# Feed-forward products of a hybrid trunk step by seven block products instead of eight: all of layer 4, the last chunk of layers 1 to 3

## Chip, cores and metric
One NeuronCore of one Trainium2 chip. The metric is the device time of one execution in microseconds (us), the median of several runs. An engine is named PE (TensorE, the matrix unit), ACT (ScalarE), DVE (VectorE), POOL (GpSimd) or SP (SyncE, which here only issues loads).

## What is computed
640 tokens (512 of a sample, 128 of a prompt) of width 1024 pass through four layers. Each has a mixer (short convolution, pooling, attention, short convolution) and a feed-forward part, both behind a norm with a modulation (shift, scale, gate) that comes from a conditioning vector. The part that the change touches:

```python
def swiglu(h, w_in, w_out):
    g, u = jnp.split(h @ w_in, 2, axis=-1)
    return (jax.nn.silu(g) * u) @ w_out
...
hp = modulate(rms_norm(xp, norm2_w[i]), mod_p[3], mod_p[4])
xp = xp + mod_p[5] * swiglu(hp, ffn_in_w[i], ffn_out_w[i])
```

`w_in` is 1024 x 5632, so there are 22 tiles of 128 gate columns and 22 of up columns: 22 pairs a layer.

## The kernel before
**Layout.** Features lie on the 128 partitions, tokens along the free axis; `h` has 8 rows of 640 tokens and two extra columns, the product of which with the weights gives the bias (642 = 320 + 322 columns). Every fp32 operand is kept as a sum of two fp32r parts, hi and lo, and a product is three passes: hi·hi, hi·lo, lo·hi (`products`, L464 and L465).

**Units and quads.** A unit is one 128-column tile of weights over 8 rows of h: 8 rows x 3 passes x 2 halves of the tokens = 48 matmuls into two PSUM banks. Its weights arrive by SP's queue in one of four raw buffers (512 KB), ACT copies them to hi (`split_hi`, L872), DVE subtracts to get lo (`split_lo`, L1236), into one of two slots. Four units make a quad. In `step(q, j)` ACT and DVE make the unit two ahead once unit j is done, since it reuses that unit's slot. Even units of a feed-forward quad are gates, odd ones are ups: `scaled_out` (L1312) multiplies a result by the inverse rms, `gate` takes silu on ACT, `times` (L1323) multiplies the two, and `g_hi_of` (L884) and `g_lo_of` (L1250) split the result for the second product.

**Chunks.** The 22 pairs go in chunks of 8, 8 and 6 pairs. Behind each chunk come two output quads (`out_quad`, 8 units), in which DVE adds gate times product to the residual x (L1360, three pieces). PE may start the unit after the next only when DVE has emptied its banks (`freed[slot]`).

**Modulation.** The next layer's modulation is computed on DVE beside the feed-forward part of layers 1 to 3: dot products of 128 x 1024 tiles (`ada_sum`, L1264), in triples of three tiles with two vectors each. POOL loads the tiles, each one once DVE has used up the tile before in its buffer (`load_ada`). In an output quad of those layers each step of DVE carries three sums (`ada_twice`, triples=2). That is POOL's only work in the kernel before, apart from a few memsets at its start.

**Order.** Each engine runs its own written-out list and is in order: a wait at the head of the list holds all behind it. In the quad before a feed-forward part (`out_quad` with squares, layer 4: after the convolution) each step also squares the row (L940), adds it to the sum of squares (L1408) and folds the norm's gain into a row of h: `fold_hi` on ACT (L927), `fold_lo` on DVE (L1389). The rms itself is taken by `rms_of` (L944) and `inverse_rms` (L1420).

Layers are counted 1 to 4 in the text and 0 to 3 in the code.

## Time and profile before
| | us |
|---|---|
| median of 3 runs (2665.64 to 2666.2) | 2665.91 |
| the profiled execution | 2665.85 |
| its span, first to last instruction | 2664.2 |
| PE busy in the span | 2651.6 (100%) |
| DVE busy | 1718.7 (65%) |
| ACT busy | 862.8 (32%) |
| POOL busy | 94.0 (4%) |

The profiled execution takes 1.65 us more than its span, and lies 0.06 us under the median. Busy time of PE merges matmuls that overlap: the duration of one (some 310 ns) is its way through the array, and the distance from one start to the next is what a matmul costs. On DVE and ACT too an instruction's duration ends somewhat after the next one can start.

### The profile page before, as it was taken

The numbers are of one execution on the slowest core, as the hardware profiler recorded it, in microseconds if no ns is written. First come the engines' busy times: TensorE is split into PE (matmuls) and PEld (weight loads), VectorE is DVE, ScalarE is ACT, GpSimd is POOL, SyncE is SP. The second block draws the span as 40 slices with busy tenths as digits, with TensorE's granted clock in tenths as the row PEclk, the third lists the DMA queues.
The fourth block names the chain that finished last, engine by engine and source line by source line (L and its number), as shares of the span: only waits on it lengthen the run. The fifth ranks groups of instructions, "written<-read, shape, count | busy, mean of one in ns | idle before, by whom it ended". The sixth has DMA issues, their size and how long they took to land.

```text
span 2664.2 us, 45828 instructions
## 1 busy us (share of the span) xinstructions
PE 2651.6 (100%) x17638; PEld 2581.8 (97%) x17638; DVE 1718.7 (65%) x2908; ACT 862.8 (32%) x1185; POOL 94.0 (4%) x185
## 2 busy tenths in 40 slices
PE   9999999999999999999999999999999999999998
PEld 5999999999999999999968999999999999999998
DVE  5898778686587777746675778676465554334345
ACT  4223332322342122125665431322332233233122
POOL 0000001000000000000000001000000000000000
PEclk9999999999999999999999999999999999999999
DMA  8443345344223444422002235443122212222212
GB/s 308 142 146 138 127 140 174 124 162 132 77 85 129 161 144 134 142 67 86 33 13 88 96 133 174 132 144 119 64 87 71 79 64 79 79 71 71 79 65 70
DMA packets 85604, 294.95 MB, mean 111 GB/s; under 512 B 10112, under 2 KB 13312, under 8 KB 85248
## 3 DMA queue, kind: packets, MB, share of 16 engines
q1 hardware_dynamic: 60016, 200.74, 22.5%
q0 software_dynamic: 25488, 92.81, 10.4%
q8 instruction: 70, 1.15, 0.2%
q14 instruction: 30, 0.25, 0.0%
HBM read 290.63 MB, written 2.88 MB: 110 GB/s over the span
## 4 chain that ended last, share of the span: by engine, by line
PE 96%; DVE 2%; ACT 1%; DMA 1%; issue 0%; DVEq 0%; ACTq 0%; SPq 0%
PE ps L464 45%; PE ps L465 45%; PE ps_x L678 1%; PE ps L654 1%; PE ps L810 1%; PE ps_sum L665 1%; DMA mix<-in_ada_head 1%; DVE w_lo L1236 1%; PE ps L761 0%; ACT w_hi L872 0%; PE ps L535 0%; PE ps_sum L640 0%; DVE g_lo L1250 0%; ACT g_hi L884 0%; DVE tmp L1312 0%
## 5 line engine op out<-in xcount | busy, mean ns | idle before, releaser
L1236 DVE TENSOR_TENSOR w_lo<-raw,w_hi 128x1024 fp32r<-128x1024 f32 (+2 forms) x359 | 429.1, 1195 | 634.0 <-ACT w_hi L872 632.0
L872 ACT ACTIVATE w_hi<-raw 128x1024 fp32r<-128x1024 f32 (+2 forms) x359 | 371.9, 1036 | 973.2 <-PE ps L465 967.1
L464 PE MATMUL ps<-h_hi,w_hi 128*128 128x320 f32 x1888 | 590.2, 313 | 0.7 <-DVE h_lo L1396 0.7
L465 PE MATMUL ps<-h_lo,w_hi 128*128 128x322 f32 x1888 | 586.5, 311 | 0.0
L464 PE MATMUL ps<-h_hi,w_lo 128*128 128x320 f32 x1888 | 586.3, 311 | 0.0
L465 PE MATMUL ps<-h_hi,w_lo 128*128 128x322 f32 x1888 | 585.8, 310 | 0.0
L465 PE MATMUL ps<-h_hi,w_hi 128*128 128x322 f32 x1888 | 584.6, 310 | 0.0
L464 PE MATMUL ps<-h_lo,w_hi 128*128 128x320 f32 x1888 | 583.9, 309 | 0.0
L1264 DVE CUSTOM_DVE_ANT_0 ps_x<-ada_w,cond 128x1024 f32<-128x1024 f32 x354 | 435.9, 1231 | 28.5 <-DVE tmp L1312 13.2
L465 PEld LDWEIGHTS ps<-h_hi,w_hi 128*128 128x128 f32 x1888 | 359.0, 190 | 0.6
L465 PEld LDWEIGHTS ps<-h_hi,w_lo 128*128 128x128 f32 x1888 | 358.2, 190 | 0.0
L464 PEld LDWEIGHTS ps<-h_hi,w_hi 128*128 128x128 f32 x1888 | 354.7, 188 | 1.5 <-DVE h_lo L1396 0.8
L465 PEld LDWEIGHTS ps<-h_lo,w_hi 128*128 128x128 f32 x1888 | 355.9, 189 | 0.0
L464 PEld LDWEIGHTS ps<-h_hi,w_lo 128*128 128x128 f32 x1888 | 355.0, 188 | 0.0
L464 PEld LDWEIGHTS ps<-h_lo,w_hi 128*128 128x128 f32 x1888 | 353.9, 187 | 0.0
L464 PE MATMUL ps<-g_hi,w_hi 128*128 128x320 f32 x884 | 274.6, 311 | 0.5
L464 PE MATMUL ps<-g_hi,w_lo 128*128 128x320 f32 x884 | 273.3, 309 | 0.0
L464 PE MATMUL ps<-g_lo,w_hi 128*128 128x320 f32 x884 | 273.2, 309 | 0.0
L465 PE MATMUL ps<-g_hi,w_hi 128*128 128x320 f32 x884 | 273.2, 309 | 0.0
L465 PE MATMUL ps<-g_hi,w_lo 128*128 128x320 f32 x884 | 273.2, 309 | 0.0
L465 PE MATMUL ps<-g_lo,w_hi 128*128 128x320 f32 x884 | 273.1, 309 | 0.0
L884 ACT ACTIVATE g_hi<-tmp 128x640 f32 (+1 forms) x104 | 76.9, 739 | 348.9 <-DVE tmp L1323 348.9
(179 smaller groups left out, 2887.9 us busy)
## 6 DMA issues: line engine op xcount, KB each, us to landing
raw<-in_weights SPq DMA_DIRECT2D x323, 512.0 KB, 3.3
ada_w<-in_ada_w POOLq DMA_DIRECT2D x177, 512.0 KB, 3.5
raw<-in_weights SPq DMA_DIRECT2D x32, 384.0 KB, 3.0
mix<-in_ada_head SPq DMA_DIRECT2D x16, 512.0 KB, 10.3
x<-in_x SPq DMA_DIRECT2D x8, 320.0 KB, 9.9
out_y<-mix SPq DMA_DIRECT2D x16, 160.0 KB, 1.9
mix<-in_spread SPq DMA_DIRECT2D x1, 1088.0 KB, 5.5
cond<-in_cond SPq DMA_DIRECT2D x1, 1024.0 KB, 13.6
```

The source lines that it names most:

```text
L464: pe.matmul(ps[:, 2 * slot, 0:TA], w[:, slot, ws], a(k)[:, 0:TA], start=begin, stop=end)
L465: mm = pe.matmul(ps[:, 2 * slot + 1, 0:width - TA], w[:, slot, ws], a(k)[:, TA:width], start=begin, stop=end)
L654: pe.matmul(out[:, 0:TS], row[:, qt * P:(qt + 1) * P], key[:, 0:TS], start=True, stop=True)
L665: mm = pe.transpose(sum_flat[:, k * P:(k + 1) * P], tmp[:, n % 2, k * P:(k + 1) * P], ident[:])
L678: pe.matmul(ps_rot, val, of_sample[:, k, :], start=(k == 0), stop=(k == 4))
L810: mm = pe.matmul(head_row[g % 2], cond_k[:, 2 * pair + k, :], head_w[:, n % HEAD_SLOTS, k * HEAD_W * P:(k + 1) * HEAD_W * P], start=(pair ...
L872: act.activation(w_hi[:, j % 2, 0:tiles * P], raw[:, j, 0:tiles * P] if src is None else src, ACT.Copy).then_inc(w_hi_ready, 1)
L884: act.activation(g_hi[:, index, :], src, ACT.Copy).then_inc(g_hi_ready, 1)
L1236: dve.tensor_tensor(w_lo[:, j % 2, 0:tiles * P], raw[:, j, 0:tiles * P] if src is None else src, w_hi[:, j % 2, 0:tiles * P].bitcast(F32), ...
L1264: dve.tensor_tensor_reduce(ada_products, ada_w[:, j * D:(j + 1) * D], cond[:, v, :], 1.0, 0.0, ALU.mult, ALU.add, ada_raw[:, j, v:v + 1]). ...
```

## The change
The gate and the up tile of a pair, each over the upper and the lower 4 rows of h, are a 2 x 2 matrix of blocks; h, by upper and lower rows and by the first and the last 322 of its columns, is another. Their product is formed by seven block products (Winograd's form of Strassen's method) in place of eight. A block product is 4 rows x 3 passes = 12 matmuls of 322 columns, all into one bank. In the code's names, with S for sums of weight blocks and T for sums of blocks of h: P1 and P2 use the gate blocks as they are, P5 to P7 and P3 use S1, S2, S3 and S4, P4 the lower up block; P1, P2 and P3 take h as it is, P5, P6, P7 and P4 take T1 to T4.

- `FIRST_SEVEN = [2, 2, 2, 0]` is the first chunk of each layer that goes by seven: the last chunk (6 pairs) of layers 1 to 3 and all 22 pairs of layer 4, 40 pairs in all. The other chunks stay as they were.
- POOL makes the four S of each pair (`s13`, `s24`, 128 x 512) and, at the beginning of a layer's first such chunk, the T of h (`t1_of`, `t234_of`, 128 x 322 each, 12 instructions for T1 and 5 for T2 to T4 of each of rows 0 to 2); DVE makes T2 to T4 of the last row (`turn_last`).
- ACT and DVE split seven blocks of 128 x 512 a pair into hi and lo (`block_hi`, `block_lo`) instead of two tiles of 128 x 1024, and split the 16 T rows (`turn_step`, in the output quad before the chunk, after the modulation sums of each step).
- There are four places for weight blocks; a block is made when the product four before it is done (`refill`). The first four blocks are made in steps 2 and 3 of the output quad before the chunk (`first_blocks`).
- Partial results leave PSUM by two copies on ACT (P1, P1+P6) and one of P5, and by adds and multiplies of 320 or 322 columns on DVE (`after_p2`, `after_p3`, `after_p4`, `after_p7`); `hidden` then multiplies gate and up as `times` did.
- Loops over the two chunks and over the output quads of a chunk are written out. SP's list is the same but for the value of one wait of layer 2.

The core of the diff (leading blanks cut, lines left out marked):

```diff
+TW = TA + 2
+HALF = KD // 2
+HW = HALF * P
...
+def _order(n):
+    out = [(0, 1), (0, 5), (0, 2), (0, 6), (0, 3), (0, 7)]
+    for p in range(1, n):
+out += [(p, 1), (p - 1, 4), (p, 5), (p, 6), (p, 2), (p, 7), (p, 3)]
+    return out + [(n - 1, 4)]
...
+FIRST_SEVEN = [2, 2, 2, 0]
...
+    def t1_of(layer, k):
+        n = 2 * layer + 1
+        pool.wait_ge(h_ready, H_BASE[n] + k + 1)
+        pool.tensor_tensor(t2_full[:, k, :], h_hi[:, k, TA:TH].bitcast(F32), h_lo[:, k, TA:TH].bitcast(F32), ALU.add)
+        own(pool.tensor_tensor(t4_full[:, k, :], h_hi[:, k, 0:TW].bitcast(F32), h_lo[:, k, 0:TW].bitcast(F32), ALU.add), steps)
+        pool.tensor_tensor(t2_full[:, k, :], t2_full[:, k, :], t4_full[:, k, :], ALU.subtract).then_inc(t1_made, 1)
+    def t234_of(layer, k):
+        n, m = 2 * layer + 1, HALF + k
+        pool.wait_ge(h_ready, H_BASE[n] + m + 1)
+        pool.wait_ge(t_lo_ready, T_STEPS * LAYER_T[layer] + k + 1)
+        own(pool.tensor_tensor(t3_full[:, k, :], h_hi[:, m, TA:TH].bitcast(F32), h_lo[:, m, TA:TH].bitcast(F32), ALU.add), steps)
+        own(pool.tensor_tensor(t2_full[:, k, :], t3_full[:, k, :], t2_full[:, k, :], ALU.subtract), steps)
+        pool.tensor_tensor(t3_full[:, k, :], t2_full[:, k, :], t4_full[:, k, :], ALU.subtract).then_inc(t2_made, 1)
+        pool.wait_ge(t2_made, HALF * LAYER_T[layer] + k + 1)
+        own(pool.tensor_tensor(t4_full[:, k, :], h_hi[:, m, 0:TW].bitcast(F32), h_lo[:, m, 0:TW].bitcast(F32), ALU.add), steps)
+        pool.tensor_tensor(t4_full[:, k, :], t4_full[:, k, :], t2_full[:, k, :], ALU.subtract).then_inc(t4_made, 1)
...
+    def s13(layer, c, p, q, n, norm):
...
+        elif c > FIRST_SEVEN[layer]:
+            pool.wait_ge(block_lo_ready, SEVEN * first)
+        pool.tensor_tensor(s1_home(p, norm), up_w[:, 0:HW], up_w[:, HW:2 * HW], ALU.add).then_inc(s_made, 1)
+        pool.wait_ge(block_lo_ready, SEVEN * first + PLACE[n][p, 1] + 1)
+        pool.wait_ge(s_made, 4 * (first + p) + 1)
+        pool.tensor_tensor(up_w[:, 0:HW], gate_w[:, 0:HW], up_w[:, 0:HW], ALU.subtract).then_inc(s_made, 1)
+    def s24(layer, c, p, n, norm):
...
+        pool.wait_ge(s_made, 4 * (first + p) + 2)
+        pool.tensor_tensor(gate_w[:, 0:HW], s1_home(p, norm), gate_w[:, 0:HW], ALU.subtract).then_inc(s_made, 1)
+        pool.wait_ge(block_lo_ready, SEVEN * first + PLACE[n][p, 2] + 1)
+        pool.wait_ge(s_made, 4 * (first + p) + 3)
+        pool.tensor_tensor(gate_w[:, HW:2 * HW], gate_w[:, HW:2 * HW], gate_w[:, 0:HW], ALU.subtract).then_inc(s_made, 1)
+    def begin_chunk(layer, c, q, n, norm, turns):
+        s13(layer, c, 0, q, n, norm)
+        if turns:
+            t234_of(layer, 2)
+        s24(layer, c, 0, n, norm)
...
+            s13(layer, c, p, q, n, norm)
+            s24(layer, c, p, n, norm)
...
+        if plain:
+            if ada:
+                with pool.Fori(t0, t0 + plain * per - 1) as i:
+                    for j in range(ADA_N):
+                        load_ada(i, j)
+            if kind == "pool":
+                pool.wait_ge(spread_done, KD)
+            pool.wait_ge(shift_ready, n + 1)
+            turn_rows(layer)
+            t234_of(layer, 0)
+            t234_of(layer, 1)
+            if ada:
+                ada_triple(t0 + plain * per - 1)
+        else:
+            if kind == "attn":
+                ada_triple(t0)
+            pool.wait_ge(shift_ready, n + 1)
+            turn_rows(layer)
...
+            begin_chunk(layer, c, qc, tiles, norm, c == FIRST_SEVEN[layer])
+            if triples and not (kind == "attn" and c == 0):
+                ada_triple(triples[0])
+            rest_of_chunk(layer, c, qc, tiles, norm, triples)
...
+        def product(p, m, out, a_hi, a_lo, begin, row_ready=None):
+            b = place[p, m]
+            pe.wait_ge(block_lo_ready, SEVEN * first + b + 1)
+            hi, lo = block_home(w_hi, n, b), block_home(w_lo, n, b)
+            for k in range(HALF):
+                if row_ready is not None:
+                    pe.wait_ge(h_ready, row_ready + k + 1)
+                ws = slice(k * P, k * P + P)
+                for i, (w, a) in enumerate(((hi, a_hi), (hi, a_lo), (lo, a_hi))):
+                    mm = pe.matmul(out, w[:, ws], a[:, k, :], start=begin and k == 0 and i == 0,
+                                   stop=k == HALF - 1 and i == 2, skip_group_check=True)
+            mm.then_inc(seven_done, 1)
...
+            pe.wait_ge(u2_kept, first + p + 1)
+            if p == 0:
+                turned_rows(T_STEPS - 1)
+            product(p, 7, bank_x(p), t3_hi, t3_lo, False)
+        p1(0)
+        p5(0)
+        p2(0)
+        if norm:
+            sum_features(sq_sum, sq_added, (KD - 1) * (row + 1), sum_ready)
+        p6(0)
+        p3(0)
+        p7(0)
+        for p in range(1, n):
+            p1(p)
...
+            p2(p)
+            p7(p)
+            p3(p)
...
+    def first_blocks(layer, c, q, j):
+        n = CHUNK if c < 2 else LAST
+        for b in {2: (0, 1), 3: (2, 3)}[j]:
+            block_hi(n, b, _pairs_before(layer, c), q, c == 0)
...
+    def t234_hi_of(layer, k):
+        act.wait_ge(t2_made, HALF * LAYER_T[layer] + k + 1)
+        act.activation(t2_hi[:, k, :], t2_full[:, k, :], ACT.Copy).then_inc(t_hi_ready, 1)
+        act.activation(t3_hi[:, k, :], t3_full[:, k, :], ACT.Copy).then_inc(t_hi_ready, 1)
+        act.wait_ge(t4_made, HALF * LAYER_T[layer] + k + 1)
+        act.wait_ge(t_lo_ready, T_STEPS * LAYER_T[layer] + HALF + 3 * k + 2)
+        act.activation(t4_hi[:, k, :], t4_full[:, k, :], ACT.Copy).then_inc(t_hi_ready, 1)
+    def turn_step(layer, j):
+        if j == 0:
+            for k in range(HALF):
+                t1_hi_of(layer, k)
+        else:
+            t234_hi_of(layer, j - 1)
...
+        if c == FIRST_SEVEN[layer]:
+            t234_hi_of(layer, HALF - 1)
+        after_p1(0)
+        after_p5(0)
...
+        after_p6(0)
+        only_refill(0, 3)
+        only_refill(0, 7)
+        for p in range(1, n):
+            after_p1(p)
+            silu(p - 1)
+            only_refill(p - 1, 4)
...
+            after_p6(p)
+            hidden_hi(p - 1)
...
             if not late:
                 step(q, j, tiles[j])
...
+                    first_blocks(*first, j)
+            if turns is not None:
...
+    def turn_last(layer):
...
+        own(dve.tensor_tensor(t2_full[:, k, :], t3_full[:, k, :], t2_full[:, k, :], ALU.subtract))
+        dve.tensor_tensor(t3_full[:, k, :], t2_full[:, k, :], t4_full[:, k, :], ALU.subtract).then_inc(t2_made, 1)
+        dve.wait_ge(t2_made, HALF * LAYER_T[layer] + k + 1)
+        own(dve.tensor_tensor(t4_full[:, k, :], h_hi[:, m, 0:TW].bitcast(F32), h_lo[:, m, 0:TW].bitcast(F32), ALU.add))
+        dve.tensor_tensor(t4_full[:, k, :], t4_full[:, k, :], t2_full[:, k, :], ALU.subtract).then_inc(t4_made, 1)
+    own_count = [0]
...
+        def after_p1(p):
+            refill(p, 1)
+            modulation(p, 0)
...
+        def after_p2(p):
+            dve.wait_ge(p1_kept, first + p + 1)
+            done(p, 2)
+            dve.tensor_tensor(gate_row(p)[:, 0:TA], gate_row(p)[:, 0:TA], bank_y(p, norm)[:, 0:TA], ALU.add).then_inc(c11_out, 1)
+            refill(p, 2)
...
+        def after_p3(p):
+            dve.wait_ge(u2_kept, first + p + 1)
+            done(p, 3)
+            dve.tensor_tensor(gate_row(p)[:, TA:TH], gate_row(p)[:, TA:TH], bank_z(p), ALU.add).then_inc(c12_out, 1)
+            dve.wait_ge(c12_out, first + p + 1)
+            dve.tensor_tensor(gate_row(p)[:, 0:T], gate_row(p)[:, 0:T], rinv, ALU.mult).then_inc(gate_scaled, 1)
...
+        def after_p4(p):
+            done(p, 4)
+            dve.tensor_tensor(up_row(p)[:, 0:TA], bank_x(p)[:, 0:TA], rinv[:, 0:TA], ALU.mult).then_inc(c21_out, 1)
...
+        def after_p7(p):
+            dve.wait_ge(p5_kept, first + p + 1)
+            done(p, 7)
+            dve.tensor_tensor(up_row(p)[:, TA:TH], up_row(p)[:, TA:TH], bank_x(p), ALU.add).then_inc(c22_out, 1)
+            dve.wait_ge(c22_out, first + p + 1)
+            dve.tensor_tensor(up_row(p)[:, TA:T], up_row(p)[:, TA:T], rinv[:, TA:T], ALU.mult).then_inc(up_scaled, 1)
...
+        if c == FIRST_SEVEN[layer]:
+            turn_last(layer)
+            t234_lo_of(layer, HALF - 1)
+        after_p1(0)
+        refill(0, 5)
+        after_p2(0)
+        if norm:
+            inverse_rms(row)
+        after_p6(0)
+        after_p3(0)
+        after_p7(0)
+        for p in range(1, n):
+            after_p1(p)
+            after_p4(p - 1)
+            refill(p - 1, 4)
+            hidden(p - 1)
+            refill(p, 5)
+            after_p6(p)
+            after_p2(p)
...
+        dve.memset(marks[:, 2:3], 0.0).then_inc(unit_done, 2 * n)
+        hidden(n - 1)
+        split_lo(q + n // 2, 1, tiles)
+        hidden_lo(n - 1)
...
+                if first is not None and j >= 2:
+                    first_blocks(*first, j)
...
+            if turns is not None:
+                turn_step(turns, j)
...
+                plain_chunk(c, at)
+            else:
...
+                out_quad(q + 1, 4, 0, gate_of(GATE2), (KD, KD, 0, 0), False, ada=last_ada, triples=2,
+                         first=(layer, c + 1, q + Q_OUT), turns=layer if c + 1 == FIRST_SEVEN[layer] else None)
...
+        if FIRST_SEVEN[layer] < 3:
+            seven_chunk(layer, 2, q, LAST, pr, g, LAST, False, [qa + ADA_Q] if layer == 0 else [])
...
```

## Rows read from the trace of the kernel before

**Rows 1.** The page: busy time, then PE and its granted clock in 40 slices.
```profile
PE 2651.6 (100%) x17638; PEld 2581.8 (97%) x17638; DVE 1718.7 (65%) x2908; ACT 862.8 (32%) x1185; POOL 94.0 (4%) x185
...
PE   9999999999999999999999999999999999999998
...
PEclk9999999999999999999999999999999999999999
```

**Rows 2.** Windows, a stretch of feed-forward units: us, PE busy (matmuls), granted clock, DMA share, GB/s.
```profile
2000.00:2100.00 100.00, 100.00 (x678) 1.00 0.22 73
```

**Rows 3.** The chain near its end: start us, us, matmuls in runs into one bank.
```profile
2641.07 7.48 PE ps L761 x51
```

**Rows 4.** DVE's timeline, last output quad before the last chunk, layer 1: start us, us, instruction.
```profile
587.43 1.23 DVE L1236 TENSOR_TENSOR w_lo<-raw,w_hi 128x1024 fp32r<-128x1024 f32 x1 [0.66 <-ACT w_hi L872]
588.57 1.13 DVE L1360 SCALAR_TENSOR_TENSOR x<-ps,mod,x 128x320 f32 x3
589.62 1.23 DVE L1264 CUSTOM_DVE_ANT_0 ps_x<-ada_w,cond 128x1024 f32<-128x1024 f32 x1
...
592.26 1.23 DVE L1264 CUSTOM_DVE_ANT_0 ps_x<-ada_w,cond 128x1024 f32<-128x1024 f32 x1
...
615.12 0.26 DVE L1304 SCALAR_TENSOR_TENSOR gain<-mod,gain 128x16 f32<-128x16 f32 x2 [0.19 <-DVE mod L1270]
```

**Rows 5.** ACT's timeline, same quad: first instruction after its last unit (L465).
```profile
607.37 1.06 ACT L872 ACTIVATE w_hi<-raw 128x1024 fp32r<-128x1024 f32 x1 [5.89 <-PE ps L465]
```

**Rows 6.** POOL's timeline, same stretch: its load behind the triple before the last two.
```profile
587.08 0.53 POOL L432 DMA_DIRECT2D ada_w<-in_ada_w  x1 [2.13 <-DVE ada_raw L1264]
```

**Rows 7.** Groups by form, DVE, ACT: busy us, mean ns of one, idle before.
```profile
L1312 DVE TENSOR_TENSOR tmp<-ps,tmp 128x640 f32<-128x640 f32 x208 | 169.4, 815 | 0.0
...
L884 ACT ACTIVATE g_hi<-tmp 128x640 f32 x94 | 69.5, 739 | 317.8 <-DVE tmp L1323 317.8
...
L1315 DVE TENSOR_TENSOR tmp<-ps,tmp 128x320 f32<-128x320 f32 x16 | 7.7, 482 | 0.0
...
L1236 DVE TENSOR_TENSOR w_lo<-raw,w_hi 128x512 fp32r<-128x512 f32 x4 | 2.7, 686 | 0.3 <-ACT w_hi L872 0.3
...
L872 ACT ACTIVATE w_hi<-raw 128x512 fp32r<-128x512 f32 x4 | 2.5, 632 | 6.2 <-PE ps L535 4.2 <-PE ps L465 1.9
```

**Rows 8.** Groups by form, POOL: its memsets of 128 and of 1 element.
```profile
L422 POOL MEMSET ones<- 128x128 f32 x1 | 0.2, 204 | 0.3 <-POOLq L1953 0.3
...
L423 POOL MEMSET eps<- 128x1 f32 x1 | 0.1, 98 | 0.0
```

**Rows 9.** DVE's timeline at the beginning of layer 4's feed-forward part.
```profile
2182.77 1.13 DVE L1360 SCALAR_TENSOR_TENSOR x<-ps,mod,x 128x320 f32<-128x320 f32 x3 [0.95 <-PE ps L465]
2183.94 1.76 DVE L1408 TENSOR_TENSOR tmp<-tmp 128x640 f32<-128x640 f32 x2
2185.61 1.01 DVE L1389 SCALAR_TENSOR_TENSOR h_lo<-x,gain,h_hi 128x512 fp32r<-128x512 f32 x2
...
2190.93 4.15 DVE L1420 RECIPROCAL tmp<-tmp 128x640 f32<-128x640 f32 x1 [3.13 <-PE ps L465]
```

**Rows 10.** ACT's timeline at the same place.
```profile
2184.58 1.00 ACT L927 ACTIVATE h_hi<-x,gain 128x512 fp32r<-128x512 f32 x2
...
2190.03 0.80 ACT L944 ACTIVATE tmp<-ps_sum,eps 128x640 f32<-128x640 f32 x1 [3.50 <-PE ps_sum L525]
2190.99 1.28 ACT L872 ACT_TABLE_LOAD   x1 [0.16 <-PE ps L465]
```

**Rows 11.** Windows at the span's end: PE, PEld, DVE, ACT, POOL busy, granted clock, DMA.
```profile
2655.00:2658.00 3.00, 2.29 (x11) 1.78 (x10) 2.42 (x7) 0.26 (x1) 0.00 (x0) 0.60 0.73 255
```

**Rows 12.** PE's timeline there: the same six matmuls (L778) at either clock.
```profile
2651.77 0.97 PE L778 MATMUL ps_x<-ident,q_scale 128*128 128x128 f32 x6
...
2656.05 1.84 PE L778 MATMUL ps_x<-ident,q_scale 128*128 128x128 f32 x6 [0.60 <-DVE q_scale L1706]
```

**Rows 13.** DMA issues: xcount, KB each, median us from issue to landing.
```profile
ada_w<-in_ada_w POOLq DMA_DIRECT2D x177, 512.0 KB, 3.5
```

More of the change, by code:

```diff
@@ L910, in out_quad @@
+            def out_quad(q, m0, n, tiles, squares, folds=True, first=None, turns=None):
                 for j in range(4):
@@ L921, in out_quad @@
                         step(q, j, tiles[j])
+                        if first is not None:
+                            first_blocks(*first, j)
+                    if turns is not None:
+                        turn_step(turns, j)
             def fold_hi(m, n):
@@ L1215, in _, with plain_chunk @@
-                ffn_in_quad(q, Q_LAST - 1, r + 2 * (Q_LAST - 1), (KD, KD, LAST, LAST))
-                q += 1
+                def plain_chunk(c):
+                    late, edge = c == 0 and kind == "pool", c == 2
+                    if c == 0 and not late:
+                        rms_of(2 * layer + 1)
+                    if late:
+                        ffn_in_quad(q, 0, r, norm=2 * layer + 1)
+                    count = Q_LAST if edge else Q_IN
+                    with act.Fori(1 if late else 0, count - 1 if edge else count) as i:
+                        ffn_in_quad(i + q, i, 2 * i + r)
+                    if edge:
+                        ffn_in_quad(q + count - 1, count - 1, r + 2 * (count - 1), (KD, KD, LAST, LAST))
@@ L1350, in out_quad @@
+            def out_quad(q, m0, n, gate, tiles, squares, folds=True, ada=None, triples=1, first=None, turns=None):
                 for j in range(4):
@@ L1354, in out_quad @@
                     if not late and not crossed:
+                        if first is not None and j >= 2:
+                            first_blocks(*first, j)
                         step(q, j, tiles[j])
@@ L1378, in out_quad @@
                     if late and tiles[j] != POOL_TILES:
+                        if first is not None:
+                            first_blocks(*first, j)
                         step(q, j, tiles[j])
@@ L1680, in attention @@
                 q += Q_QKV
+                seven = FIRST_SEVEN[layer] == 0
                 for half in range(Q_OUT):
@@ L1683, in attention @@
                         shift_lo(2 * layer + 1)
-                    out_quad(q + half, 4 * half, 2 * layer + 1, gate_of(GATE1), (KD,) * 4, True)
+                    out_quad(q + half, 4 * half, 2 * layer + 1, gate_of(GATE1), (KD, KD, 0, 0) if half and seven else (KD,) * 4, True,
+                             first=(layer, 0, q + Q_OUT) if half and seven else None, turns=layer if half and seven else None)
             def tail(q, gate):
```

432 lines of the change are left out of this document (370 added, 62 removed).

## The prediction, made before the changed kernel was run

> **What bounds the kernel now.** The page first: PE is busy 100% of the span, DVE 65%, POOL 4%, and PE's granted clock is full in all 40 slices [rows 1]. So a matmul taken out of PE's list is time gained, as long as the others keep up. What one costs is not its duration but the distance of the starts: 678 matmuls in 100 us are 147.5 ns each [rows 2], and where one bank takes many in a row it is 7.48 / 51 = 146.7 ns for 320 columns [rows 3], so twelve into one bank cost nothing more. Then the timelines where the new chunks begin. Layer 1's last output quad shows the engine that is nearly full: in 7.0 us a step DVE does a split (1.14 us to the next start), an x update (1.05) and three modulation sums of 1.32 each, [rows 4], 6.2 us.
>
> **What PE saves.** A pair is 96 matmuls before and 7 x 12 = 84 after, all of 322 columns at 147.5 ns [rows 2]: 14.13 and 12.39 us, 1.74 less. A block product is 1.77 us. 40 pairs give **-69.6 us**.
>
> **Do the others keep up, in the middle of a chunk?** An instruction here lets the next start some 0.09 us before its own end (1.23 against 1.14, [rows 4]). DVE, per pair: seven block splits at 0.686 less 0.09 [rows 7], 4.2; four results of 320 columns at 0.40 [rows 7], 1.6; one of 318, 0.4; the gates by the inverse rms, 0.73; `hidden` 1.0, as the same two pieces take in [rows 9]; lo of the result 0.75; waits on itself 0.3: **9.0 of 12.39 us**. ACT: seven splits at 0.57 [rows 7], three copies 1.3, silu 1.0 (two pieces, as [rows 10]), hi 0.7: 7.0 us. In order of time nothing comes late: the tightest is P7, which waits for the copy of P1+P6 with only P2 (1.77 us) between, and that copy takes 0.5. A block has three products (5.3 us) for 0.63 + 0.69 us of splits. SP's loads keep their distance: 1 MB per 12.4 us, landing in some 3.5 us each as [rows 13]. I take nothing for the middle.
>
> **What POOL's instructions cost.** None like them is in the trace. Its memsets take 204 ns for 128 elements and 98 for one [rows 8], 0.835 ns an element for one pass over 128 lanes. With two inputs and an output the low bound is one pass (0.37 us for 322 elements, 0.53 for 512), the high one three passes behind each other (0.90, 1.38). I take 2.5 passes, as the inputs are two of the three and the write should partly overlap: **0.77 and 1.17**. The Trainium skill (GPSIMD Engine Reference, § 3.1) has 4497 ns for a two-input add of 2048 elements; by proportion 0.71 and 1.12, and the sum below would be 3 us lower.
> Per pair POOL has four, 4.7 of 12.4 us: hidden.
>
> **The beginning of the last chunk in layers 1 to 3.** Here the sum is decided. Time 0 is the end of the quad's last unit (607.3, [rows 5]); before, PE goes on at once. After, in mid-case:
> - POOL is free for T at -19.7, since it first issues the second-last triple of loads (587.08 + 0.53, [rows 6]). Twelve instructions: T1 is ready at -10. ACT and DVE stand in step 0's `turn_step` until then. DVE's own step 0 would be over at -13.7 (592.26 + 1.33).
> - DVE's step 1 is late: split visible -7.4, x update -6.3, sums -2.4, T row 0 to -0.5. POOL makes rows 0 and 1 until -1.6, issues the last triple (three times 0.53) and S1 at +1.2.
> - Step 2: the second block needs S1: lo at +2.4. Behind it stands the x update (3.5) that frees P1's bank: PE is idle 3.5 us. Sums to 7.5, T row 1 to 9.4 (two lo's 0.9, hi of T4 0.5, its lo 0.5, each waiting for the other engine).
> - Step 3: ACT, held by row 1, makes blocks three and four; DVE's lo's at 10.8, x 12, sums 16.2, T row 2 18.1, gains 0.5 [rows 4] 18.6, the five instructions of `turn_last` at 0.5 each 21.2, lo of T2 and T3 22.1. ACT then makes the hi of T4 and only behind that copies P1: 23.1.
> - P6 waits for that copy. Without stall it would start after P1, P5, P2, at 5.3. **Stall 18 us**, three times: **+54**. From P6 on nothing waits.
> POOL at its low price gives 13 (DVE then sets it), at its high one 21.5. Were no step late at all, DVE's work behind 0 alone (splits 1.9, x 1.1, sums 4.2, T row 1.9, gains 0.5, `turn_last` 2.6, splits and copy 1.9) ends at 14.1: 9 is the floor.
>
> **Layer 4's first chunk** (0 is 2182.7, [rows 9]) has no modulation, but the norm. POOL starts at -21.8, T1 -12, rows 0 and 1 -1.3, S1 0. The second block's lo is there at 1.2, x 2.3: PE starts 2.3 late. Last row of h: x update 8.0 (DVE comes from T row 1), two adds 9.6 (1.76 for both, [rows 9]), fold 10.7, blocks 12, T row 2 13.8, `turn_last` 16.4, copy of P1 18.3. Against 6.2 (5.3 and 0.85 for the norm's sum) that is 12 us. Then ACT's table load and root (1.28 and 0.80, [rows 10]) stand before the copy that P7 wants, 1.3; and the reciprocal of 4.15 us [rows 9] stands before the result that P4 waits for, 3.2. With 1 us of waits there before: **+16** (floor 10). Layer 4's other two chunks need no T: their S2 comes in time, 0.
>
> **The clock.** These are idle times of some 10 us for PE. The trace has short ones at its end: among small matmuls with a gap of 0.6 us [rows 12] the granted clock of 2655 to 2658 is 0.60 [rows 11], partly at 1.2 GHz, and six matmuls take 1.84 us where they took 0.97 [rows 12]. How long a fall lasts no row shows: from nothing to three products at twice their time (5.3 us) a place. I take 1.5, by four places **+6**.
>
> **Sum:** -69.6 + 54 + 16 + 6 = +6.4. From the profiled execution's 2665.85 that is 2672.3; the median of the runs shown is 0.06 higher, so **2672 us**. What a measurement of this kernel tells from no change is 0.2%, 5.3 us.
>
> **Rivals.**
> - *Faster: the beginnings cost less.* With POOL's low price 3 x 13 + 12, and a clock that falls for less time (2): -69.6 + 53 = -17, 2649. With the floors alone, 27 + 10, and no fall, 2633. For it: four steps of my chain depend on POOL's price. Against: DVE's 14 us behind the last unit stand whatever POOL takes. It decides for faster from 16 us a place downwards in layers 1 to 3.
> - *Slower: POOL and DVE hold each other up.* Nothing in the trace shows DVE beside a computing POOL, so this is open. In an output quad of layers 1 to 3 DVE has 0.8 us free in 7; 22 T instructions of 0.77 and three S are 20 us in the same 28. If only one of the two engines could read at a time, half of that (it waits anyway in the rest) would come on top at each of four places, +40; in the middle of a chunk 9.0 + 4.7 less what lies beside PSUM reads (1.0) is 12.7, 0.4 a pair over PE, +16: 2672 + 56 = 2728.
>  The Trainium skill (SBUF — State Buffer, § Who interferes with whom) states just this: a DVE instruction with two SBUF inputs and a GpSimd instruction that reads SBUF exclude each other for a whole instruction, and by it 2728 would be the result. No row here shows it.
> - *The saving isn't there:* if twelve matmuls at other weights in one bank cost 160 ns, pairs save 0.7 us, and it ends at 2714. [Rows 3] speaks against it.
>
> **Chances.** The forecast (2659 to 2690) 0.42; the beginnings cheaper 0.27; engines that hold each other up 0.27; no saving 0.04. Limits are 2660.6 and 2671.2. Faster by over 0.2%: the second case and a small part of the first, 0.30. Within: 0.17, from the lower half of the first. Slower: 0.53. The range 2643 to 2728 leaves out the floors alone, and what lies above the rule's sum.
>
> **What would show it.** Windows in the middle of a chunk: PE 100% busy at 147 ns a matmul, granted clock 1.00. At the four beginnings: PE idle, P6's wait put down to the copy of P1 on ACT or to the lo of T2; the window's clock under 1. POOL's adds at 0.77 and 1.17, and DVE's splits of 512 at 0.69; if these are longer beside POOL's than elsewhere, the second rival holds. The forecast is wrong if the four places sum to under 55 us, or if PE waits in every pair.

## The result, and the profile after

The changed kernel takes **2736.6 us** (median of 4 runs, 2736.26 to 2737.99) where the kernel before takes 2665.8: **2.7% slower**, ratio 1.0266 [1.0253, 1.028]. The forecast was 2672, its range ended at 2728, and the slower rival stood at 2728. The direction was right, though only just forecast (6 us slower, with a chance of 0.53); the size was not.

The page of the profiled execution (2736.26 us, span 2734.6), its lines that answer to [rows 1]:
```profile
PE 2621.4 (96%) x17158; PEld 2545.8 (93%) x17158; DVE 2033.4 (74%) x3337; ACT 968.3 (35%) x1538; POOL 464.2 (17%) x453
...
PE   9999999996999999889999999997899997999998
...
PEclk9999999997999999989999999998999998999999
```
480 matmuls fewer, as the change says (40 pairs by 12). But PE is no longer at 100%. Its idle time is 2734.6 - 2621.4 = 113.2 us, before it was 12.6: **+100.6**. Its busy time fell by 30.2 where the 480 matmuls are worth 69.6, so **+39.4** lies in matmuls that took longer (most of it at the lower clock, see experiment 4). -69.6 + 100.6 + 39.4 is the +70.4 between the two spans. In the row of 40 slices PE dips at four places, and the clock's row dips with it: these are the beginnings of the chunks by seven.

What PE waited for (engine, line, releaser: us in total, times, longest us):
```profile
PE ps L754 <- ACT tmp L1299: 33.5, 4, 10.2
PE ps L754 <- DVE x L1991: 23.0, 4, 6.5
PE ps L700 <- DVE x L1991: 21.8, 4, 6.4
PE ps_sum L754 <- issue: 10.8, 3, 3.7
PE ps L754 <- issue: 6.3, 1, 6.3
```
L754 is the block product, L700 a plain one, L1299 the copy of P1, L1991 the x update. "4 times" is once a place. The steps that the prediction named all stand here: P6 behind the copy of P1, P1 behind the x update that frees its bank, P2 (`ps_sum`) behind the split of its weight block (in layer 4 behind the last row of h, the 6.3 us). One wait the prediction does not have: L700 is here the last unit of the output quad, which waits for an x update too, 6.4 us in each of layers 1 to 3 and 2.6 in layer 4. By place the waits sum to 29.6, 26.0, 25.8 and 18.1 us in layers 1 to 4.

The chain of layer 1's beginning shows how they came about (start us, us, what). Without a stall the quad's last unit ends between 608.1 and 608.5, as in experiments 2, 6 and 7: that is the prediction's time 0. Here this unit only starts then, and ends at 616.87:
```profile
607.97 0.61 PE L700 MATMUL ps<-g_hi,w_hi 128*128 128x320 f32 x1 [6.38 <-DVE x L1991]
```
```profile
605.78 1.74 POOL mix L566
...
607.59 0.86 POOL mix L568
...
608.53 1.74 POOL mix L569
610.27 1.83 POOL mix L564
...
618.86 1.28 POOL tmp L592
...
622.01 1.12 DVE x L1991 x3
623.13 1.73 DVE ps_x L1730
...
629.57 1.48 DVE h_lo L1840
...
639.11 1.88 DVE h_lo L1840
...
642.32 0.42 DVE mix L1861
...
646.25 0.43 ACT tmp L1299
646.73 6.43 PE ps L754 x24
```
It is the forecast chain in the forecast order: POOL makes T rows 0 and 1, then S1 (L592), the second block is split, the x update frees the bank, the modulation sums (L1730) and T splits (L1840 is one) follow, then `turn_last` (L1861), and ACT's copy of P1 (L1299) comes last. Only it ends at 646.73 instead of about 631: the same instruction on 322 columns takes 0.86 on POOL once and 1.74 to 1.83 at other times, and a split of the same size that DVE does in 0.48 takes 1.48 or 1.88.

### The profile page after: what moved, and what is told of

It is laid out like the page before. It is cut to its first block, busy times and chain, and to the rows that moved or that the text cites. A ratio compares the mean times of both kernels' runs of the same rounds, so it can differ in the third digit from the quotient of the medians.

```text
span 2734.6 us, 45243 instructions
## 1 busy us (share of the span) xinstructions
PE 2621.4 (96%) x17158; PEld 2545.8 (93%) x17158; DVE 2033.4 (74%) x3337; ACT 968.3 (35%) x1538; POOL 464.2 (17%) x453
## 4 chain that ended last, share of the span: by engine, by line
PE 82%; DVE 9%; POOL 4%; issue 3%; ACT 2%; DMA 1%; DVEq 0%; ACTq 0%; POOLq 0%; SPq 0%
PE ps L700 32%; PE ps L701 32%; PE ps L754 12%; PE ps_sum L754 2%; DVE w_lo L1817 1%; DVE ps_x L1730 1%; PE ps_x L1010 1%; PE ps L986 1%; POOL mix L554 1%; PE ps L1142 1%; POOL mix L555 1%; PE ps_sum L997 1%; POOL mix L556 1%; DVE tmp L1935 1%; DMA mix<-in_ada_head 1%
## 5 line engine op out<-in xcount | busy, mean ns | idle before, releaser
L1730 DVE CUSTOM_DVE_ANT_0 ps_x<-ada_w,cond 128x1024 f32<-128x1024 f32 x354 | 452.2, 1277 | 31.9 <-DVE tmp L1778 11.6
L700 PE MATMUL ps<-h_hi,w_hi 128*128 128x320 f32 x1248 | 390.4, 313 | 0.7 <-DVE h_lo L2031 0.7
L701 PE MATMUL ps<-h_lo,w_hi 128*128 128x322 f32 x1248 | 388.8, 312 | 0.0
L701 PE MATMUL ps<-h_hi,w_lo 128*128 128x322 f32 x1248 | 387.9, 311 | 0.0
L700 PE MATMUL ps<-h_lo,w_hi 128*128 128x320 f32 x1248 | 387.9, 311 | 0.0
L700 PE MATMUL ps<-h_hi,w_lo 128*128 128x320 f32 x1248 | 387.6, 311 | 0.0
L701 PE MATMUL ps<-h_hi,w_hi 128*128 128x322 f32 x1248 | 386.8, 310 | 0.0
L700 PE MATMUL ps<-g_hi,w_hi 128*128 128x320 f32 x884 | 276.3, 313 | 22.2 <-DVE x L1991 21.8
L700 PE MATMUL ps<-g_hi,w_lo 128*128 128x320 f32 x884 | 274.4, 310 | 0.0
L700 PE MATMUL ps<-g_lo,w_hi 128*128 128x320 f32 x884 | 274.4, 310 | 0.0
L754 PE MATMUL ps<-turned,w_hi 128*128 128x322 f32 x960 | 224.4, 322 | 38.3 <-ACT tmp L1299 33.5
L701 PEld LDWEIGHTS ps<-h_hi,w_hi 128*128 128x128 f32 x1248 | 236.6, 190 | 0.5
L701 PEld LDWEIGHTS ps<-h_hi,w_lo 128*128 128x128 f32 x1248 | 236.7, 190 | 0.0
L700 PEld LDWEIGHTS ps<-h_hi,w_hi 128*128 128x128 f32 x1248 | 235.3, 189 | 1.3 <-DVE h_lo L2031 0.8
L700 PEld LDWEIGHTS ps<-h_hi,w_lo 128*128 128x128 f32 x1248 | 236.0, 189 | 0.0
L701 PEld LDWEIGHTS ps<-h_lo,w_hi 128*128 128x128 f32 x1248 | 235.3, 189 | 0.0
## 6 DMA issues: line engine op xcount, KB each, us to landing
mix<-in_ada_head SPq DMA_DIRECT2D x16, 512.0 KB, 10.3
```

The lines of the kernel that those rows point to most:

```text
L700: pe.matmul(ps[:, 2 * slot, 0:TA], w[:, slot, ws], a(k)[:, 0:TA], start=begin, stop=end)
L701: mm = pe.matmul(ps[:, 2 * slot + 1, 0:width - TA], w[:, slot, ws], a(k)[:, TA:width], start=begin, stop=end)
L754: mm = pe.matmul(out, w[:, ws], a[:, k, :], start=begin and k == 0 and i == 0, stop=k == HALF - 1 and i == 2, skip_group_check=True)
L1730: dve.tensor_tensor_reduce(ada_products, ada_w[:, j * D:(j + 1) * D], cond[:, v, :], 1.0, 0.0, ALU.mult, ALU.add, ada_raw[:, j, v:v + 1]). ...
```

## Why instructions double: one timeline

DVE and POOL in the last output quad before that beginning (start us, us, engine, instruction):
```profile
590.58 0.88 POOL L555 TENSOR_TENSOR mix<-h_hi,h_lo 128x322 f32<-128x322 f32 x1
590.83 1.72 DVE L1730 CUSTOM_DVE_ANT_0 ps_x<-ada_w,cond 128x1024 f32<-128x1024 f32 x1
591.53 1.75 POOL L556 TENSOR_TENSOR mix<-mix 128x322 f32<-128x322 f32 x1
...
592.64 1.73 DVE L1730 CUSTOM_DVE_ANT_0 ps_x<-ada_w,cond 128x1024 f32<-128x1024 f32 x1
593.24 1.86 POOL L554 TENSOR_TENSOR mix<-h_hi,h_lo 128x322 f32<-128x322 f32 x1
```
Read the ends. The first of these adds of POOL ends at 591.46. DVE's sum began at 590.83, but ends 1.09 after that point, at 592.55. POOL's next began at 591.53 and ends at 593.28, 0.73 after DVE's end. DVE's next ends at 594.37, 1.09 after 593.28. So they work by turns, and each instruction's time holds the rest of the other's: a sum of 1.23 [rows 4] shows 1.72, an add of 0.87 shows 1.75 or 1.86. The groups show the same, and also which instructions are spared (busy us, mean ns of one):
```profile
L1817 DVE TENSOR_TENSOR w_lo<-raw,w_hi 128x512 fp32r<-128x512 f32 x240 | 206.0, 880 | 37.6 <-ACT w_hi L1252 35.7
L1941 DVE TENSOR_TENSOR g_lo<-tmp,g_hi 128x640 fp32r<-128x640 f32 x40 | 60.0, 1500 | 0.0
L1935 DVE SCALAR_TENSOR_TENSOR tmp<-tmp 128x512 f32<-128x512 f32 x40 | 53.6, 1339 | 3.2 <-ACT tmp L1320 3.2
...
L1902 DVE TENSOR_TENSOR tmp<-tmp,ps 128x322 f32<-128x322 f32 x40 | 19.4, 484 | 0.9 <-PE ps L754 0.9
```
The split of 512 took 686 ns [rows 7] and takes 880. L1902, with one input from PSUM, takes 484, as its like did (482, [rows 7]). The Trainium skill (SBUF — State Buffer, § Who interferes with whom) gives just this rule, a lock held for a whole instruction between a DVE instruction with both inputs in SBUF and a GpSimd one that reads SBUF; the trace agrees, with these numbers.

## The experiments

**1. The parts alone.** The plan of chunks is one line, so each part can be run without the other.
```
-FIRST_SEVEN = [2, 2, 2, 0]
+FIRST_SEVEN = [3, 3, 3, 0]      (a1_layer4)
+FIRST_SEVEN = [2, 2, 2, 3]      (a2_last_chunks)
```


> Only layer 4 goes by seven (its 22 pairs), layers 1 to 3 as before. From the trace of the changed kernel: 22 pairs save 38.3 us, PE's waits in layer 4 are 18 us, its pairs come every 12.83 us where 84 matmuls need 12.39 (about 18 pairs, +8), and 17 us of low clock cost some 4. If the loss is made where the last chunks of layers 1 to 3 begin, this kernel is faster than before: 2658 us (2650 to 2665). If layer 4 loses as well, it is above 2671.

> Only the last chunks of layers 1 to 3 go by seven, layer 4 as before. If the two parts simply add, this one is 2736.6 less what layer 4 brings: 2744 us (2736 to 2752), with three places of 26 to 30 us of waits and 100 us at the low clock.

Measured: layer 4 alone 2658.5 us, ratio 0.9972 [0.9962, 0.9983], so **7.3 us gained**. The last chunks alone 2747.4 us (a single run), **81.6 lost**. Both are as expected. 18 pairs are worth 31.3, so the three places cost (81.6 + 31.3) / 3 = 37.6 us each, where the prediction has 19.5 with the clock. Layer 4's 22 pairs are worth 38.3; 31 of it is lost. The prediction has 17.5 there. (Not all of either is lost at a beginning: experiment 6 shows 4 us that every changed kernel loses in its plain units.)

**2. POOL's arithmetic taken out.** Every add of the block sums becomes a memset of the same tile, with the same waits; no sum is made. POOL's instructions stay in number and order, but read nothing.
```
-pool.tensor_tensor(t2_full[:, k, :], t2_full[:, k, :], t4_full[:, k, :], ALU.subtract)
+pool.memset(t2_full[:, k, :], 0.0)          (and so the other eleven lines)
```


> All of POOL's adds and subtractions (the S of the weights, the T of h) are replaced by memsets of the same outputs with the same waits and signals: what is left out is the sums themselves; POOL reads nothing and is shorter. If POOL and DVE exclude each other when both read SBUF, DVE's splits of 512 fall from 0.88 to 0.69 us and its last lo split from 1.50 to 0.82, pairs of layer 4 come every 12.4 us, and the time is 2650 to 2672, as my sum with the low price of POOL and the clock added. If only the order of the lists counts and not POOL, DVE's durations stay and the time stays over 2710.

Measured 2651.9 us (a single run, as are those of experiments 3 and 4). The groups that had stretched are back to their lengths:
```profile
L1817 DVE TENSOR_TENSOR w_lo<-raw,w_hi 128x512 fp32r<-128x512 f32 x240 | 164.2, 690 | 111.4 <-ACT w_hi L1252 108.8
...
L1935 DVE SCALAR_TENSOR_TENSOR tmp<-tmp 128x512 f32<-128x512 f32 x40 | 29.9, 746 | 3.2 <-ACT tmp L1320 3.2
...
L1941 DVE TENSOR_TENSOR g_lo<-tmp,g_hi 128x640 fp32r<-128x640 f32 x40 | 32.8, 820 | 0.0
```
So the adds are worth 84.7 us. (A memset is also shorter than an add, 0.37 us for 322 columns and 0.53 for 512 where an add with no DVE instruction beside it takes 0.88 and 1.28. So this is the adds' own length and the holding-up together, and no run parts them. As an estimate by the prediction's own figures, 13 us a place with cheap adds and some 21 with adds of 0.87, the length is about 8 of the 21 us a place.) That it is the reading and not the mere running of POOL is seen within the traces: in the changed kernel the 72 splits of 512 that have an add beside them for 0.3 us or more take 1336 ns in the mean, those with none 684; here 53 have a memset beside them so long and take 691, those with none 690. Where they cost it is seen by laying the copies of P1 of both kernels side by side: at the first of layer 1 this kernel is 21.1 us ahead, at the last 26.5, at the last of layer 3 67.3, at the first of layer 4 82.9, at its last 84.2. So the beginnings have nearly all of it, and layer 4's pairs next to nothing (1.3).

Something is left that POOL has no part in: 2651.9 against 2665.9 - 69.6 = 2596.3 is 55.6 us, 14 a place. Its waits are P6's, all but unchanged:
```profile
PE ps L754 <- ACT tmp L1299: 32.8, 4, 10.3
```
That the longest of them stays 10.3 while 85 us vanish is a lesson in reading waits: P6's wait begins when P2 is done. In the changed kernel PE came to it late, after two stalls at the x update. Those are gone here, and the copy of P1 comes at 625.13 instead of 646.25.

**3. Which sums.** The same with the sums of the weights (S) alone, and with those of the hidden state (T) alone.

> Only the block sums of the weights (four adds a pair, 128x512, on POOL) become memsets of the same homes; the sums of the hidden state stay. If the pairs' middle is where POOL hurts: the 16 pairs of the fourth layer fall from 12.82 to 12.50 us, some 7 us less, and the start of each chunk gets back only the four sums of its first pair, some 3 us each: 2717 us. If the sums of the weights hold up the starts as well as the sums of the hidden state do, 2700 or less. If the two kinds share one cause, beside each other, the gains of this kernel and its twin add up to more than the 84 us of the kernel without either.

> Only the block sums of the hidden state (eight adds a row of blocks, four rows, 128x322, on POOL, at the four starts) become memsets; the sums of the weights stay. If the starts are where the time went: nearly all of the 84 us come back, 2670 us (2660 to 2685), and the wait of P6 for the copy of P1 goes from 10 us to nothing or stays only as far as DVE's own list is late. If the middle of the chunk costs the most, it stays above 2700.

Measured 2715.4 and 2671.4: the S sums are worth 21, the T sums 65, and together 86 (experiment 2: 85). The T sums are two fifths of the adds (108 of 268) and three quarters of the damage, because they stand where PE waits. The total for S was as expected, its place was not. By the copies of P1 the kernel without S sums is ahead by 4.2 us at the first of layer 1, 9.8 at its last, 16.7 at the last of layer 3, 21.1 at the first of layer 4, 19.7 at its third and 21.0 at its last. So S costs at the beginnings too, and in layer 1's pairs, and in layer 4's only 1.3.

The copies of P1 in layer 1 of the changed kernel show what happens in pairs (ACT's timeline: start us, us, instruction):
```profile
656.80 0.44 ACT L1299 ACTIVATE tmp<-ps 128x320 f32<-128x320 f32 x1 [1.22 <-PE ps L754]
670.85 0.44 ACT L1299 ACTIVATE tmp<-ps 128x320 f32<-128x320 f32 x1 [1.21 <-PE ps L754]
687.02 0.44 ACT L1299 ACTIVATE tmp<-ps 128x320 f32<-128x320 f32 x1 [1.20 <-PE ps L754]
699.52 0.44 ACT L1299 ACTIVATE tmp<-ps 128x320 f32<-128x320 f32 x1 [1.21 <-PE ps L754]
```
12.50 us is the distance wherever a pair goes well, in layer 4 too. PE waits for nothing in it: a matmul of a block product starts 148.8 ns after the one before, not 147.5, and 84 of them are 12.50. In layer 1 the first two distances shown are 14.05 and 16.17: in its first two pairs DVE has three modulation sums besides (the triple that only this layer has). Without the S sums these two distances are 12.55 and 12.75, so the modulation sums alone do not slow the pairs, the two together do. In layer 4 DVE's own rounds are longer than PE's, 12.82 us from one `hidden_lo` to the next (2312.44, 2325.26). It falls behind by 0.32 a pair, and the slack of the waits takes this up until the last pair of a chunk of eight, whose distance is 12.83 (12.50 without the S sums).

**4. The clock.** PE's waits had brought low clocks, so the question was what these cost. Dummy products of `ones` were put into PE's list ahead of its waits:
```
+if turns and not norm:
+    warm(WARM_AT[norm][2])      (44 matmuls of 128 columns, whose result nobody reads; 15 to 26 at the other places)
 p6(0)
```


> Matmuls of ones that nobody reads are put into PE's list ahead of its long waits (8 us ahead of P6, 3 to 5 ahead of the others), and nothing else is changed; they fill waits and add no work to another engine. If the low clock behind the waits costs some 30 us, the mean granted clock rises from 0.977 to 0.99 or more and the time falls to 2705 to 2718. If the clock is only a sign of the waits and costs little, the time stays within 5 us of 2736.

Measured 2735.3 us, 1.3 less. The windows of layer 1's beginning in the changed kernel, then here (us; PE, PEld, DVE, ACT, POOL busy; granted clock; DMA):
```profile
600.00:615.00 15.00, 8.62 (x48) 8.38 (x48) 10.83 (x15) 2.73 (x5) 14.41 (x12) 0.77 0.11 36
615.00:630.00 15.00, 8.11 (x37) 7.59 (x35) 11.20 (x15) 2.35 (x5) 14.37 (x14) 0.77 0.30 105
630.00:645.00 15.00, 3.56 (x12) 3.18 (x12) 13.40 (x26) 3.54 (x8) 5.19 (x6) 0.57 0.34 105
645.00:660.00 15.00, 11.93 (x61) 11.66 (x62) 13.98 (x23) 6.76 (x14) 4.02 (x3) 0.75 0.20 71
```
```profile
600.00:615.00 15.00, 14.40 (x111) 14.24 (x110) 10.11 (x14) 2.73 (x5) 14.37 (x13) 1.00 0.11 37
615.00:630.00 15.00, 12.85 (x91) 12.66 (x90) 11.20 (x15) 2.35 (x5) 14.37 (x14) 0.89 0.28 106
630.00:645.00 15.00, 13.95 (x121) 13.79 (x121) 13.46 (x25) 3.11 (x8) 5.96 (x6) 1.00 0.37 106
645.00:660.00 15.00, 9.12 (x60) 8.66 (x59) 13.92 (x24) 7.20 (x16) 3.81 (x2) 0.98 0.22 70
```
The clock is at its upper level nearly throughout, and nothing is won. In 645 to 660 PE has as many matmuls as before (60 and 61), done in 9.12 instead of 11.93 us, and it waits the rest: the wait for a result of DVE in the second pair (`tmp`) grows from 1.3 to 3.9 us. DVE's list set the pace in any case. The lower clock as a cost (a gain of 18 to 31 us, to 2705 to 2718) was wrong; the other case, within 5 us of 2736, held. Of the +39.4 above some 28 us are the lower clock (an estimate: some 240 matmuls that follow each other at 267 ns instead of 147), and they lay in time that PE would have waited. What the dummy products themselves held up is not parted from this; the first copies of P1 behind them come 0.8 and 0.7 us later in layers 1 and 2, earlier in layers 3 and 4.

**5. The same work, begun earlier.** Layers 1 to 3 with another order: POOL starts T ahead of its last two triples of loads, T1 of rows 0 and 1 is split a step earlier, POOL makes the last row as well, the copy of P1 goes ahead of the last row's splits, and the last two triples' modulation sums move into the chunk's pairs.
```
+s13(layer, 2, 0, qc, LAST, False, (1,))     (POOL: S1 first)
 t234_of(layer, 0)
+ada_triple(last)
 t234_of(layer, 1)
...
-turn_last(layer)                            (DVE: the last row now on POOL)
+copy_p1(0)                                  (ACT)
 t234_hi_of(layer, HALF - 1)
```


> The whole sums stay, but the starts of the three last chunks are ordered anew: POOL begins the sums of the hidden state ahead of its loads of the modulation weights, T1 of rows 0 and 1 is split a quad earlier, DVE's sums of the last two triples of modulation move out of the last quad into the chunk's pairs, and the copy of P1 goes ahead of the last row's splits. The fourth layer is as before the change. Theory (each start is a fixed list on POOL and DVE that holds each other up, which can lie elsewhere): the three waits of 26 to 30 us shrink to some 3 each, 2646 us (2636 to 2665), against 2747 for the same three chunks in the order of the change. Rival (the time is lost to POOL and DVE together wherever the sums lie): over 2700.

> As its twin, with the fourth layer's feed-forward by seven products too, in the order of the change. The fourth layer alone gave 7.3 us, so 7 us under its twin: 2638 us (2628 to 2658) if the starts are the cause; over 2695 if the rival holds.

Measured 2725.3 us, ratio 1.0223 [1.0206, 1.0241], and 2711.5, 1.0173 [1.0156, 1.019]: 22 and 25 us better than with the change's order, far from the 100 that I had expected. The waits alone don't tell why; the copies of P1 do. Layer 1's first is at 621.48, where the changed kernel has 646.25, so the beginning did get 25 us shorter. But the pairs, which now hold the modulation sums, are slow. In layer 2:
```profile
1189.02 0.42 ACT L1331 ACTIVATE tmp<-ps 128x320 f32<-128x320 f32 x1
1205.04 0.44 ACT L1331 ACTIVATE tmp<-ps 128x320 f32<-128x320 f32 x1 [1.21 <-PE ps L777]
```
A distance of 16.02 instead of 12.50. From first to last copy it is 77.3 us, and 60.7 in the changed kernel: 16.6 lost in the pairs of layer 2, 11 in layer 1 and 18 in layer 3.

**6. T made a chunk ahead.** The hidden state is there from the feed-forward's start, so T needn't wait for the last quad. POOL makes T1 in the first chunk's quads in, T2 to T4 in the second chunk's, one row behind each load. Only the splits of T3 and T4 must stay in the last quad, since T3's home is free no earlier.
```
+def _turns_at(layer, c, quad, j):
+    first = FIRST_SEVEN[layer]
+    if first == 2:
+        return {(0, 0): [(1, j)], (1, 0): [(2, j)], (1, 1): [(3, j), (4, j)]}.get((c, quad), [])
...
+t1_of(layer, 0)
+t1_of(layer, 1)
+triples_to(2, 3)
...
+for k in range(HALF):
+    t234_of(layer, k)
+    triples_to(9 + k, 10 + k)
```
The same for layer 4 is possible only from its second chunk on (`FIRST_SEVEN[3] = 1`); its first chunk stays plain. Three kernels: [2, 2, 2, 3], [2, 2, 2, 1] and [3, 3, 3, 1].

> The last chunks of layers 1 to 3 by seven products, the fourth layer as before the change. The sums and splits of the hidden state no longer stand at the chunk's start: POOL makes T1 in the first chunk's quads in and T2 to T4 in the second chunk's, one row behind each load of a triple; T1 is split in the first chunk's first quad out, T2 in the second chunk's first quad out, T3 and T4 in its last one (T3's home in the hidden state is free only by then). The modulation sums stay where they were. Theory (the 82 us of the three starts are work that stands too late, and is free where DVE and POOL have room): 18 pairs by 1.74 are 31 us saved, each start keeps some 3 to 6 us of waits, 2647 us (2640 to 2660). Rival (the adds cost the same wherever they stand, since they hold DVE up there too): over 2700, as in the kernel whose sums begin only a little earlier (2725).

> As its twin, and of the fourth layer the second and third chunk (14 pairs) by seven products, with the sums and splits of its hidden state in the first chunk and its quads out; the first chunk stays plain, so no sum stands between the norm and the first product. Theory: 14 pairs by 1.74 save 24, less 0.3 a pair for the sums of the weights in the pairs and some 3 us at the start, 17 us under its twin: 2630 us (2620 to 2645). If the fourth layer's gain hangs on its 22 pairs, no more than 7 under the twin.

> Only the fourth layer's second and third chunk by seven products, the three last chunks as before the change: 17 us under the kernel before, 2649 us (2642 to 2658), if a start with the sums made early costs some 3 us; 2658 or more (what the whole fourth layer gave) if it costs 12 as the first chunk's start did.

| plan | us | ratio to before |
|---|---|---|
| [2, 2, 2, 3], T early | 2677.6 | 1.0043 [1.0026, 1.0059] |
| [2, 2, 2, 1], T early | 2655.8 | 0.9961 [0.9946, 0.9975] |
| [3, 3, 3, 1], T early | 2648.2 | 0.9933 [0.9916, 0.9949] |

The first gets back 69.8 of the 81.6 us with the same adds and modulation sums, the adds only elsewhere. (The splits of T1 and T2 moved with them, and the last row's five adds went from DVE to POOL; their share is not parted.) That decides against "the adds cost the same wherever they stand". But it isn't the 2647 expected: 18 pairs should give 31.3 and it is 11.7 slower, so 14.3 us are left at each place. That is what was left with POOL's adds taken out (14). Its waits:
```profile
PE ps L779 <- ACT tmp L1337: 16.9, 3, 5.9
PE ps_sum L779 <- issue: 8.2, 3, 2.7
```
(L779 is the block product, L1337 the copy of P1.) Layer 1's first copy is at 621.42, 9 us later than with no stall. The second is 21.8 us under the first, more than the 17 expected between them, though not at the 2630 that was expected with it.

The third is as expected (2649), and it is **faster than both kernels**: 17.7 us under the kernel before. 14 pairs are worth 24.4, so 6.7 are lost. Its waits for block products come to next to nothing:
```profile
PE ps L779 <- ACT tmp L1337: 0.6, 1, 0.6
```
Where the 6.7 lie is read by laying PE's timelines side by side, the kernel before and then this one, at the start of layer 4's second chunk and at the first output product behind its last pair:
```profile
2353.84 0.31 PE L464 MATMUL ps<-h_hi,w_hi 128*128 128x320 f32 x1
...
2609.23 0.31 PE L464 MATMUL ps<-g_hi,w_hi 128*128 128x320 f32 x1
```
```profile
2358.24 0.31 PE L779 MATMUL ps<-h_hi,w_hi 128*128 128x322 f32 x1
...
2591.50 0.31 PE L725 MATMUL ps<-g_hi,w_hi 128*128 128x320 f32 x1
```
The stretch takes 255.39 us before and 233.26 here, so 22.1 are saved and 2.3 lost in it. Behind it nothing is lost: both kernels have 55.0 us left to their spans' ends. The other 4.4 us are lost ahead of it, where no pair goes by seven. They grow evenly, 0.25 to 0.33 us in each chunk of plain pairs: a plain matmul over h starts 148.3 ns after the one before, where it was 147.9 in the kernel before, while those over g keep their 146.7. Every changed kernel has this. What the edit changes for these matmuls is the length of h's rows (`ROW = T + 8` where it was `T + 4`, room for T3); that this is the cause was not tested.

**7. The modulation sums spread over the pairs.** The last try at layers 1 to 3: the 12 modulation sums of the last quad at two a pair (three in layer 1).
```
+if e < 2:
+    i = 2 * p + e
+    ada_share(ada[i // 6], i % 6, i % 6 + 1)
```


> As the kernel with early sums and the fourth layer's second and third chunk (2655.8 us), with the modulation sums of the last two triples moved from the last quad ahead of each last chunk into the chunk's six pairs, two sums a pair (three in layer 1, which has a third triple), and their loads on POOL one slot at a time. Theory (what is left of the three starts, some 14 us each, is DVE's list, which holds 12 modulation sums of 1.37 us in the quad in which it also splits T3 and T4 and the first blocks): the starts fall to 3 to 5 us, 2627 us (2620 to 2640). Rival (the list is full in the chunk's pairs too: 9.0 of 12.4 us and 2.7 more of sums, before any stretching beside POOL, as the kernel with these sums in fewer pairs showed with 7 us of waits in its middle): the time goes to the pairs, 2645 us or more.

Measured 2656.7 us, ratio 0.9966 [0.9953, 0.9978]: no better than with these sums in the quad (2655.8). Layer 1's first copy of P1 is at 612.35, as early as without any stall, 9.1 before the kernel with these sums in the quad. So the stall that experiment 6 left was theirs. The pairs take it back (layer 2, two sums a pair):
```profile
1134.73 0.42 ACT L1342 ACTIVATE tmp<-ps 128x320 f32<-128x320 f32 x1
1148.63 0.44 ACT L1342 ACTIVATE tmp<-ps 128x320 f32<-128x320 f32 x1 [1.20 <-PE ps L784]
1162.27 0.42 ACT L1342 ACTIVATE tmp<-ps 128x320 f32<-128x320 f32 x1
```
13.90 and 13.64 instead of 12.50, then 14.23 and 16.06, and in layer 1, with three sums, 15.65 to 18.25. A window there shows DVE full (14.97 of 15 us, the third busy time):
```profile
675.00:690.00 15.00, 13.32 (x81) 13.05 (x80) 14.97 (x21) 6.98 (x13) 8.38 (x6) 0.90 0.55 190
```
The rival held. By the figures so far a pair has 9.0 us of DVE's own work and 12.82 with its turns; 2.7 more has no room in 12.4.

## Why the prediction was wrong

- **The saving** (-69.6) and **"nothing" for the middle**: the count is right, the price of a matmul a little off. By the prediction's own 147.5 ns a pair before is 14.16 us and not 14.13. Start to start the traces have 147.9 ns before (14.20 a pair) and 148.8 in a block product (12.50), so a pair saves 1.70 and 40 pairs 68. Layer 1's two slow pairs add 5.2, and the plain units over h, which the prediction took as unchanged, some 3 (4.4 in the last kernel of experiment 6). Small errors, some 10 us together.
- **What POOL's instructions cost**: the lone prices 0.77 and 1.17 measure 0.87 and 1.28, between my choice and the high bound (0.90, 1.38). By the prediction's own figures (13, 18 and 21.5 for the three prices) that is some 3 us a place. The proportion worked out from the Trainium skill (GPSIMD Engine Reference, § 3.1), 0.71 and 1.12, lies further below.
- **The step that failed is the overlap of POOL and DVE, whose cost to each other the sum put at nothing.** POOL's and DVE's durations were laid beside each other as if each had the memory to itself, in the very quad where the prediction had DVE at 6.2 us of 7 and POOL busy throughout. The copy of P1 was to come at +23.1 and came at +37.8. In layer 4 it was to come at +18.3 and came at +28 (2214.94 with layer 4 alone, where time 0 is 2186.6, since the plain units ahead have lost 4 us). So the stalls were 33 and 22 us, not 18 and 12. Part of it shows as a wait that the prediction has nowhere, the quad's last unit behind an x update: 21.8 us over the four places. Taking the adds out gave 84.7 us, nearly all at these places. The rival that named it had 0.27 and deserved more.
- **The rival's own size** (+40 at the beginnings, +16 in the pairs, 2728) came near the total but was split wrongly. It took half of POOL's time as the surcharge, 10 a place. It was 15 in layers 1 to 3, some 3 of them the longer adds themselves: every row of T that comes late also delays the x update queued behind it in DVE's list, and this raised the stall for P1's bank from 3.5 to between 6.3 and 6.5 us and made the one of 6.4 ahead of the quad's last unit. In the pairs its 12.7 us for DVE and POOL together were nearly right (12.82), but the conclusion, 0.4 a pair for PE (0.3 by its own figures, so 12 us and not 16), was not: DVE falls behind inside the slack of the waits. Six pairs don't use it up, and of eight only the last shows it, with 0.33. Otherwise PE feels it only with modulation sums besides.
- **The clock** (+6): it fell more often and for longer than I took, and lifting it brought 1.3 us, no more than the runs of the changed kernel differ among themselves (2736.26 to 2737.99). The term was wrong in kind: here the slow products lay in time that PE waited in any case.
- **The floors** (9 and 10 us a place, "DVE's 14 us behind the last unit stand whatever POOL takes"): confirmed in kind, low in size; with no adds 14 a place are left (about 1 of it in plain units and pairs), and experiment 7 shows that in layer 1 at least 9 of them are the modulation sums.

What stays open: why plain matmuls over h take 0.4 ns longer in every changed kernel (4.4 us in the fastest), and how the 84.7 us part into the adds' length and the turns. And no run has a last chunk whose modulation sums go neither into the quad before it nor into its pairs (earlier quads in have room, 21 to 24 us busy of 30), so whether six pairs could pay in layers 1 to 3 wasn't tried.

## What to carry to other kernels

Before giving POOL arithmetic, look at what DVE reads in that stretch: if it is mostly two SBUF inputs, add the two engines' times instead of taking the larger. Sums that depend only on data which has long been there belong where both engines have room; here the same adds in three layers, with half of their splits, cost 70 us more at the chunk's edge than a chunk earlier. Work moved away from a full stretch needs a place with room, or it costs the same there: that has to be counted per pair, with the turns in it. To find where time is lost, lay one repeated instruction or one transition of both kernels side by side: that showed 4.4 us in stretches that nobody meant to change, which no list of waits shows. And a cheaper algorithm with a fixed entry cost should be used where the run behind the entry is long: 14 pairs behind one cheap entry won 17.7 us, 6 pairs behind a dear one lose.
